# Taking the transpose and value steps of prompt attention two groups at a time

## The chip, the cores and the metric

The kernel runs on one core of a Trainium2 chip. The metric is the device time of the whole launch in microseconds, as the median of several runs. One execution was also profiled; all rows of the trace below come from it. Times in a row are counted from the first instruction of that execution.

## What is computed

One inference step of a hybrid decoder layer for a prompt of 2048 tokens and a group of 8 short samples. Three mixers stand side by side: A, a dilated sliding-window attention with 6 heads of 64; B, a gated linear recurrence (RG-LRU) after a short convolution; C, a chunked gated recurrence (HGRN2). The change touches only A, and only for the prompt:

```python
def dilated_branch_prompt(q, k, v, window, dilation):
    ...
    scores = jnp.einsum('brnqhd,brnkhd->brnhqk', qb, kband, ...) * (dh ** -0.5)
    ...
    scores = jnp.where(valid[:, None], scores, -jnp.inf)
    mx = jnp.max(scores, axis=-1, keepdims=True)
    p = jnp.exp(scores - mx)
    l = jnp.sum(p, axis=-1, keepdims=True)
    o = jnp.einsum('brnhqk,brnkhd->brnqhd', p, vband.astype(jnp.float32)) / jnp.swapaxes(l, 3, 4)
```

Three such branches (window, dilation) = (128, 1), (512, 4), (2048, 16) are merged with weights proportional to their denominators. Everything is in float32.

## The kernel before, in words

The program has two parts. `front` normalizes the input, projects it and runs the two recurrences. `attend_project` computes the attention of the prompt (and, at its start, the recurrence C of the samples and the last value columns), then the attention of the samples and the output projection. The change is in `attend_schedule`, which writes out by hand one list of steps, `order`. Each engine runs through that same list in one loop and does its own part of each step, so the list fixes the order on every engine's queue. Waits between engines are semaphores.

The steps that matter here:

- **u** (192 of them, 32 for each head): the scores of one tile of 128 queries against 128 to 512 keys. TensorE does two matmuls (L2545, L2546) into one of three PSUM banks (`a_s`); VectorE adds the mask and takes the row's extreme (L2306), which frees the bank: score step n waits at L2537 until step n-3 was shifted. ScalarE then takes the exponential and the row sum (L2167). In a head, unit k of 32 is: four of 128 keys, four near ones (128 or 256), then four of 256, four near, four of 384, four near, four of 512, four near.
- **w, x, z** (once for each head): the statistics of the far keys are sent across partitions. After the last exponential of the head VectorE makes `a_exch` (L2230), TensorE spreads it with eight small matmuls (x, L2594), VectorE and ScalarE merge, TensorE spreads the result (z, L2602), and VectorE copies the weights (L2367). GpSimd then scales the head's probabilities with them (L2082), in ten instructions.
- **t** (108 of them, 18 for each head): one group of four 128x128 blocks of probabilities is transposed by TensorE (L2613) into one of two PSUM banks (`a_t`). ScalarE copies three groups of four to SBUF (L1677), VectorE the fourth (n with n % 4 == 3, L1679), into one of four buffers `a_pt`.
- **o** (108): the four transposed blocks of a group are multiplied with the values (L2636), in 128*64 tiles of TensorE, two column halves side by side; 8 matmuls in the trace for 4 blocks. It waits for the copy of its group.
- **f** (12): VectorE multiplies a finished half of a head with its gate (L2377) and SyncE stores it.
- **pw** (9): ScalarE rounds a slab of the output weights (L2178), VectorE takes the rest (L2383). SyncE loads the slabs into four buffers; slab n+4 is loaded when pw n is over. **pt**: TensorE transposes a tile of the mixed rows for the projection (L2696), after it was loaded from DRAM.

The groups trail the scores: a head's groups begin LEAD = 11 score steps after its last score step. After each one or two score steps from there on, the inner function `turn` appends one t step, the o step of two groups before, and an f step where one is due. So in the middle of the kernel the list reads, for one head's stretch: u81 u82 t22 o20 u83 t23 o21 u84 u85 t24 o22 u86 u87 t25 o23. After the last score step (u191) come the 24 groups that are left, with the steps x, z, pw and pt between them.

Of the kernel before, what the change touches and what calls it, by code (L numbers as in the profile page):

```python
# [1388 lines left out]
def project_schedule():  # L1389

    first = [32 * b // 10 + 4 for b in range(NB)]
    at = {}
    for b, s in enumerate(first):
        for step, kind in enumerate(("sk", "sm", "so")):
            at[s + step] = (kind, b)  # L1400
    order = []
    for s in range(2 * NTILE):
        i, h = s // 2, s % 2
        kind, b = at.get(s, ("", 0))
        if h == 0 and i:
            order.append(("pt", i + 1))
        if at.get(s + 1, ("",))[0] == "sk":
            order.append(("sr", at[s + 1][1]))
        if kind == "sk":
            order.append(("ss", b))  # L1410
        order.append(("pp", s))
        if s == 0:
            order.append(("pt", 1))
        if s == 1:
            order.append(("sq", 0))
        if kind:
            order.append((kind, b))
        if at.get(s - 1, ("",))[0] == "so":
            order.append(("sb", at[s - 1][1]))
        order.append(("pe", s))  # L1420
        if s < 3:
            order.append((("si", "sj", "sl")[s], 0))
        tail = [("sc", b), ("sx", b), ("sn", b)] if kind == "sk" else []
        done = [("pf", i), ("pg", i), ("ph", i)] if h else []
        order += [x for pair in itertools.zip_longest(tail, done) for x in pair if x]
    n = 2 * NTILE
    return order + [("pp", n), ("pe", n), ("pp", n + 1), ("pe", n + 1)] + [(k, NTILE) for k in ("pf", "pg", "ph")]
# [10 lines left out]
def block_keys(i, far, m):  # L1438

    if far:  # L1440
        return list(range(i + 1))
    return [j for j in (NC * i + m, NC * i + m - 1) if j >= 0]
# [6 lines left out]
def last_group(groups, h, i):  # L1449
    return max(t for t, (g, blocks) in enumerate(groups) if g == h and any(b[0] == i for b in blocks))  # L1450


def attend_schedule():

    units = [(h, i, far, m) for h in range(NH) for i in range(SB) for far in (1, 0) for m in range(NC)]
    groups = []
    for h in range(NH):
        rows = [[(i, far, a, j) for i in both for far in range(2) for a in range(NC) for j in block_keys(i, far, a)] for both in LANES]
        blocks = [b for pair in itertools.zip_longest(*rows) for b in pair if b]
        groups += [(h, blocks[b:b + 4]) for b in range(0, len(blocks), 4)]  # L1470
    per, gper = len(units) // NH, len(groups) // NH
    ends = [max(last_group(groups, h, both[step]) for both in LANES) for h in range(NH) for step in range(2)]
    halves = [(h, j) for j in range(J0, XTILES) for h in ("va", "vb")]
    order, made = [], 0
    for step in ("ha", "va", "vb", "hb", "va", "hp", "qa", "ht", "hc", "vb", "hd", "va", "vb", "hx", "va"):
        order.append(halves.pop(0) if step[0] == "v" else (step, 0))
    order.append(("qa", 1))
    hgrn = {0: [("hk", 0), ("he", 0)], 1: [("hz", 0), ("hp", 1)], 2: [("ht", 1), ("hp", 2)], 3: [("ht", 2), ("hp", 3)],
            4: [("ht", 3), ("hj", 0)], 5: [("hj", 1)], 9: [("lk", 1)], 11: [("hq", 0), ("hv", 0)],
            12: [("hr", 0), ("hv", 1)], 13: [("hn", 0)]}  # L1480
    for h in range(NH):
        hgrn.setdefault(5 + h, []).append(("ho", h))
        if h < NH - 2:
            hgrn.setdefault(6 + h, []).append(("hj", h + 2))
    later = {2: [("hu", 0)], 3: [("hu", 1), ("hv", 2)], 5: [("hu", 2), ("hv", 3)], 6: [("hu", 3), ("hv", 4)],
             7: [("hu", 4), ("hv", 5)], 9: [("hu", 5)], 10: [("hs", 0)]}

    def turn():
        nonlocal made
        order.append(("t", made))  # L1490
        if made >= 2:
            order.append(("o", made - 2))
        if made - 3 in ends:
            order.append(("f", ends.index(made - 3)))
        made += 1

    for u in range(len(units)):
        h, k = u // per, u % per
        order.append(("u", u))
        if h == 0 and k % 2:  # L1500
            order += hgrn.get(k // 2, [])
            if halves:
                order.append(halves.pop(0))
            if k + 1 == per:
                assert not halves
                order += [("ve", 0), ("qa", 2), ("qa", 3)]
        if h == 1:
            order += later.get(k, [])
        if h and h + 1 < NH:
            order += {2: [("lk", h + 1)], 12: [("qn", 2 * h + 2)], 18: [("lv", 1)] * (h == 1), 22: [("qn", 2 * h + 3)]}.get(k, [])  # L1510
        if h and k in (1, 4):
            order.append(("x" if k == 1 else "z", h - 1))
        if k + 1 == per:
            order.append(("w", h))
        done = u + 1 - per - LEAD
        while done >= 0 and made < done // per * gper + done % per * gper // per + 1:
            turn()
    left = (NH - 1) * gper - made
    for n in range(left):
        turn()  # L1520
        if n in (1, 3):
            order.append(("x" if n == 1 else "z", NH - 1))
    order.append(("pl", 0))
    for n in itertools.count():
        if 4 <= n < 4 + KM:
            order.append(("pw", n - 4))
        if n == 11:
            order.append(("pm", 0))
        if n == 16:
            order.append(("pt", 0))  # L1530
        if made == len(groups):
            break
        turn()
    order += [("o", made - 2), ("o", made - 1), ("f", len(ends) - 1)]
    return units, groups, ends, order + project_schedule()


def attend_project(nc, sem, io, con, zf, zt, zs, mt, mab):

    units, groups, ends, order = attend_schedule()
    PER = len(units) // NH
    NCH = NH // 2
# [1256 lines left out]
```

## Time and profile before

| | |
|---|---|
| Median of 3 runs | 1688.76 us (1685.87 to 1689.35) |
| Profiled execution, first to last instruction | 1690.4 us |
| Its own time beside that span | not given apart from the span |
| TensorE matmul busy | 1588.9 us, 94% |
| TensorE weight load busy | 1345.8 us, 80% |
| VectorE busy | 976.2 us, 58% |
| ScalarE busy | 823.9 us, 49% |
| GpSimd busy | 628.9 us, 37% |
| Mean granted TensorE clock | 0.969 |
| Stretch with t and o steps | 1180 to 1376 us |

The busy shares are means over stages with different limits; what the change is worth is read from the stretch from 1180 to 1376 us. PE is TensorE's matmuls, PEld its weight loads, which overlap the matmuls; DVE is VectorE, ACT ScalarE, POOL GpSimd, SP SyncE. A matmul's duration in the trace covers its way through the array, so neighbours overlap: the distance from start to start says what one costs. "Idle before" in square brackets is how long the engine stood still ahead of the row, with what ended it; "issue" there means that nothing was waited for that the profile shows.

### The profile page before, as it was taken

The page shows a single profiled execution, that of the slowest core. Times are in us where ns is not written, and L with a number is a line of the kernel's source. Part 1 is how long each engine was busy: PE and PEld are TensorE (multiplying, and loading weights), DVE is VectorE, ACT ScalarE, POOL GpSimd, SP SyncE. Part 2 cuts the span into 40 slices and gives each one's busy share as a digit, 9 for nine tenths or more (in the row PEclk, how much of TensorE's full clock was granted, in tenths as well). Part 3 has the DMA queues.
Part 4 walks back from the last instruction along what each step waited for, and adds up shares of the span by engine and source line. Part 5 has one row for each costly group of instructions (what it writes and reads, how often), then busy time and mean ns, then how long its engine had stood idle before and what let it go on. Part 6 is the DMA issues. An engine that isn't in the chain of part 4 may idle for free. (4 is left out here: it accounts for less than half of the span.)

```text
span 1690.4 us, 38531 instructions
## 1 busy us (share of the span) xinstructions
PE 1588.9 (94%) x15345; PEld 1345.8 (80%) x15345; DVE 976.2 (58%) x2066; ACT 823.9 (49%) x1603; POOL 628.9 (37%) x754
## 2 busy tenths in 40 slices
PE   6999998899999999999999998899999888999997
PEld 5988887889988888878888787886777667777775
DVE  3436763433377777677676776325666556555652
ACT  4426876212256555566767776244777631111110
POOL 1102221200076666666666665203645602121110
PEclk9999998999999999999999999897999989999999
DMA  6310111124412212121110211447993284775651
GB/s 212 114 51 29 34 39 59 50 73 135 141 38 62 57 36 79 41 75 30 56 46 26 67 31 43 118 112 178 239 237 85 78 258 127 247 229 189 208 171 47
DMA packets 196287, 175.27 MB, mean 104 GB/s; under 512 B 84915, under 2 KB 180686, under 8 KB 193806
## 3 DMA queue, kind: packets, MB, share of 16 engines
q1 hardware_dynamic: 196110, 172.82, 35.6%
q8 instruction: 122, 2.00, 0.5%
q14 instruction: 55, 0.45, 0.1%
HBM read 123.18 MB, written 52.84 MB: 104 GB/s over the span
## 5 line engine op out<-in xcount | busy, mean ns | idle before, releaser
L49 PE MATMUL f_bank<-c_ht,c_whi 128*128 128x384 f32 (+1 forms) x864 | 321.0, 372 | 5.7 <-DVE c_wlo L893 5.7
L51 PE MATMUL f_bank<-c_ht,c_wlo 128*128 128x384 f32 (+1 forms) x864 | 303.3, 351 | 0.0
L50 PE MATMUL f_bank<-c_ht,c_whi 128*128 128x384 f32 (+1 forms) x864 | 302.9, 351 | 0.0
L842 ACT ACTIVATE f_scr<-f_scr 128x384 f32<-128x384 f32 (+1 forms) x210 | 114.0, 544 | 206.3 <-POOL f_scr L617 206.2
L1056 DVE TENSOR_TENSOR f_scr<-f_scr 128x192 f32<-128x192 f32 (+1 forms) x210 | 105.4, 502 | 137.4 <-ACT f_scr L842 137.1
L49 PEld LDWEIGHTS f_bank<-c_ht,c_whi 128*128 128x128 f32 x864 | 162.7, 188 | 21.4 <-DVE c_wlo L893 6.5
L50 PEld LDWEIGHTS f_bank<-c_ht,c_whi 128*128 128x128 f32 x864 | 163.2, 189 | 9.7 <-issue 1.1
L51 PEld LDWEIGHTS f_bank<-c_ht,c_wlo 128*128 128x128 f32 x864 | 163.0, 189 | 9.4
L616 POOL TENSOR_TENSOR f_scr<-f_scr 128x192 f32<-128x192 f32 (+1 forms) x210 | 134.6, 641 | 40.7 <-PE f_tps L1240 37.8
L1047 DVE COPY_PREDICATED f_scr<-f_scr,f_tps 128x384 f32<-128x384 int32 (+1 forms) x210 | 130.6, 622 | 18.1 <-PE f_tps L1240 9.5
L49 PE MATMUL a_s<-a_whi,a_mhi 128*128 128x512 f32 (+1 forms) x306 | 125.8, 411 | 4.5 <-DVE a_y L2471 4.5
L50 PE MATMUL a_s<-a_wlo,a_mhi 128*128 128x512 f32 (+1 forms) x306 | 122.4, 400 | 0.0
L642 POOL TENSOR_SCALAR f_scr<-f_scr,c_lbl 128x384 f32<-128x384 f32 (+1 forms) x30 | 43.5, 1451 | 209.7 <-ACT f_scr L808 209.7
L1240 PEld LDWEIGHTS f_tps<-f_scr 128*32 128x32 f32 (+1 forms) x5184 | 74.3, 112 | 40.0 <-issue 30.4
L1240 PE MATMUL f_tps<-f_scr 128*32 128x32 f32 (+1 forms) x5184 | 95.6, 200 | 2.5 <-DVE f_scr L1056 2.4
L2102 POOL TENSOR_TENSOR a_small<-a_small,c_mhalf 128x1 f32<-128x1 f32 (+1 forms) x17 | 9.3, 544 | 235.4 <-DVE a_small L2475 235.4
L49 PE MATMUL f_bank<-c_whi,c_ht 128*128 128x384 f32 x256 | 92.3, 360 | 2.2 <-DVE c_wlo L897 2.2
L51 PE MATMUL f_bank<-c_whi,c_ht 128*128 128x384 f32 x256 | 88.2, 344 | 0.0
L50 PE MATMUL f_bank<-c_wlo,c_ht 128*128 128x384 f32 x256 | 88.2, 344 | 0.0
L49 PE MATMUL f_bank<-c_htail,c_whi 128*128 128x448 f32 x216 | 84.3, 390 | 0.0
L51 PE MATMUL a_s<-a_whi,a_mlo_a 128*128 128x512 f32 (+1 forms) x204 | 82.0, 402 | 0.0
L50 PE MATMUL f_bank<-c_htail,c_whi 128*128 128x448 f32 x216 | 79.3, 367 | 0.0
(401 smaller groups left out, 3816.2 us busy)
## 6 DMA issues: line engine op xcount, KB each, us to landing
f_wraw<-in_w_in SPq DMA_DIRECT2D x27, 512.0 KB, 4.0
zs<-f_stage SPq DMA_DIRECT2D x48, 192.0 KB, 2.4
a_k<-in_ck SPq DMA_DIRECT2D x48, 192.0 KB, 5.7
a_v<-in_cv SPq DMA_DIRECT2D x48, 192.0 KB
f_scr<-in_xp SPq DMA_DIRECT2D x16, 512.0 KB, 4.2
a_x<-in_xp SPq DMA_DIRECT2D x16, 512.0 KB, 5.6
out_y_prompt<-a_y SPq DMA_DIRECT2D x16, 512.0 KB, 2.9
zt<-f_stage SPq DMA_DIRECT2D x38, 192.0 KB, 1.8
```

Source lines behind the costliest of these rows:

```text
L49: nc.tensor.matmul(out, w_hi, m_hi, start=start, stop=False)
L50: nc.tensor.matmul(out, w_hi, m_lo, start=False, stop=False)
L51: return nc.tensor.matmul(out, w_lo, m_hi, start=False, stop=stop)
L616: G.tensor_tensor(d[:, :, hs:], b[:, :, hs:], r, ALU.subtract)
L642: G.tensor_scalar(key[:, :n], key[:, :n], lbl[:, 1, h:h + 1], None, ALU.mult).then_inc(S["gated"], 1)
L842: A(lev[i % 3][:, :n], lev[i % 3][:, :n], ACT.Exp).then_inc(S["expd"], 1)
L1047: V.copy_predicated(attn[:, :n].rearrange("p (j t) -> p j t", t=P), m.bitcast(I32).unsqueeze(1).to_broadcast([P, nt, P]), lp[x % 2][:, :n] ...
L1056: V.tensor_tensor(e[:, :, hs:], e[:, :, hs:], q[:, :, hs:], ALU.mult).then_inc(S["xlev"], 1)
L1240: mm = nc.tensor.matmul(lp[x % 2][k0:k0 + w, queries], left[:, keys], right[:, queries], start=True, stop=True)
L2102: G.tensor_tensor(s[:, 2:3], s[:, 1:2], con["mhalf"][:rows_of(n), 0:1], ALU.pow).then_inc(Z["rstd"], 1)
```

## The change

`turn` handles two groups at once: two t steps, then the two o steps of the two groups before, then the f steps due. It is called half as often. The number and kind of instructions stay the same, and so do the buffers; only the order in the queues changes. The scores that stood between two single turns now stand together, so three or four score steps come in a row: u81 u82 u83 t22 t23 o20 o21 u84 u85 u86 u87 t24 t25 o22 o23.

```diff
+    assert gper % 2 == 0
+
     def turn():
         nonlocal made
-        order.append(("t", made))
+        order.extend(("t", made + x) for x in range(2))
         if made >= 2:
-            order.append(("o", made - 2))
-        if made - 3 in ends:
-            order.append(("f", ends.index(made - 3)))
-        made += 1
+            order.extend(("o", made - 2 + x) for x in range(2))
+        order.extend(("f", ends.index(n)) for n in (made - 3, made - 2) if n in ends)
+        made += 2
 
     for u in range(len(units)):
...
-        while done >= 0 and made < done // per * gper + done % per * gper // per + 1:
+        while done >= 0 and made + 1 < done // per * gper + done % per * gper // per + 1:
             turn()
     left = (NH - 1) * gper - made
     for n in range(left):
-        turn()
+        if n % 2 == 0:
+            turn()
         if n in (1, 3):
             order.append(("x" if n == 1 else "z", NH - 1))
...
         if made == len(groups):
             break
-        turn()
+        if n % 2 == 0:
+            turn()
     order += [("o", made - 2), ("o", made - 1), ("f", len(ends) - 1)]
```

Around the exchange of a head (here head 2) the list before is u93 u94 t29 o27 u95 w2 u96 t30 o28 u97 x2 u98 t31 o29; after the change it is u91 u92 u93 u94 t28 t29 o26 o27 f2 u95 w2 u96 u97 x2 u98 t30 t31 o28 o29. Near the end the list before is t94 o92 pw1 t95 o93 pw2 t96 o94 pw3 t97 o95; after the change it is pw0 t94 t95 o92 o93 pw1 pw2 t96 t97 o94 o95 pw3 pw4.

## Rows read from the trace of the kernel before

**Rows 1.** Busy time by stage: head 1's groups, the fourth of four heads, the tail.
```profile
core 0: us, PE busy (x) PEld busy (x) DVE busy (x) ACT busy (x) POOL busy (x), PEclk, DMA share, GB/s
1180.01:1203.61 23.60, 23.52 (x187) 18.92 (x187) 13.48 (x50) 17.92 (x53) 13.77 (x7) 0.89 0.97 217
...
1299.54:1331.66 32.12, 32.12 (x301) 24.86 (x301) 20.07 (x83) 25.52 (x80) 16.72 (x10) 1.00 0.08 18
1331.66:1376.34 44.68, 33.88 (x296) 24.39 (x295) 25.52 (x33) 18.30 (x28) 17.68 (x10) 0.81 0.55 176
```

**Rows 2.** Waits from 1203 to 1330 us: total, times, longest.
```profile
PEld a_o L2636 <- issue: 11.4, 68, 0.2
...
PEld a_s L2545 <- DVE a_sn L2306: 3.4, 20, 0.2
```

**Rows 3.** Timeline of TensorE: start, duration, instruction; a turn between near scores.
```profile
1209.19 0.38 PE L2545 MATMUL a_s<-a_khi,a_qn 128*128 128x256 f32 x1
...
1209.54 0.28 PE L2545 MATMUL a_s<-a_khi,a_qn 128*128 128x256 f32 x1
...
1209.77 0.60 PE L2613 MATMUL a_t<-c_ident,a_pf 128*128 128x128 f32 x4
1210.30 0.66 PE L2636 MATMUL a_o<-a_pt,a_vf 128*64 128x128 f32 x8
1210.89 0.38 PE L2545 MATMUL a_s<-a_khi,a_qst 128*128 128x256 f32 x1
```

**Rows 4.** Timeline: a turn without scores, and the last three o steps.
```profile
1342.51 0.65 PE L2613 MATMUL a_t<-c_ident,a_pnb 128*128 128x128 f32 x4
...
1343.68 0.44 PE L2613 MATMUL a_t<-c_ident,a_pnb 128*128 128x128 f32 x2
...
1373.51 2.79 PE L2636 MATMUL a_o<-a_pt,a_vf 128*64 128x128 f32 x22
```

**Rows 5.** Timeline: from a score's start to the start of its exponential, 256 keys.
```profile
1304.71 0.38 PE L2545 MATMUL a_s<-a_khi,a_qn 128*128 128x256 f32 x1
...
1305.90 0.51 ACT L2167 ACTIVATE a_pnb<-a_pnb,a_sn 128x256 f32<-128x256 f32 x1
```

**Rows 6.** The same with 512 keys.
```profile
1229.88 0.50 PE L2545 MATMUL a_s<-a_khi,a_qst 128*128 128x512 f32 x1
...
1231.57 0.73 ACT L2167 ACTIVATE a_pf<-a_pf,a_sf 128x512 f32<-128x512 f32 x1 [0.87 <-DVE a_sf L2306]
```

**Rows 7.** Timeline: a head's last score, its exponential, the exchange on VectorE and TensorE.
```profile
1297.31 0.39 PE L2545 MATMUL a_s<-a_khi,a_qn 128*128 128x256 f32 x1
...
1298.57 0.49 ACT L2167 ACTIVATE a_pnb<-a_pnb,a_sn 128x256 f32<-128x256 f32 x1
...
1299.19 0.29 DVE L2230 TENSOR_TENSOR a_exch<-a_sf,a_quarter 128x128 f32<-128x128 f32 x1 [0.72 <-ACT a_pnb L2167]
...
1299.54 0.27 PE L2594 MATMUL a_x<-a_exch,a_unit_row 128*32 128x32 f32 x8
```

**Rows 8.** Timeline of the tail: VectorE, TensorE.
```profile
1345.95 7.67 DVE L2383 TENSOR_TENSOR a_wlo<-a_wraw,a_whi 128x1024 fp32r<-128x1024 f32 x2 [2.18 <-ACT a_whi L2178]
...
1353.54 0.68 DVE L1679 COPY a_pt<-a_t 128x512 f32<-128x512 f32 x1
...
1354.37 0.45 PE L2613 MATMUL a_t<-c_ident,a_pnb 128*128 128x128 f32 x1 [5.92 <-DVE a_pt L1679]
```

**Rows 9.** The chain that ended last, from 1354 to 1363 us.
```profile
1354.22 1.14 DVE a_wlo L2383
...
1355.38 4.58 DMA a_wraw<-in_w_out
...
1362.21 1.16 DVE a_oa L2377
```

**Rows 10.** Timeline of TensorE in the projection: small matmuls after a wait.
```profile
1475.96 1.19 PE L2513 MATMUL a_o<-a_selm,a_far_rows 128*96 128x16 f32 x12 [1.69 <-DVE a_far_rows L2418]
```

**Rows 11.** The stretch behind Rows 10, columns as in Rows 1.
```profile
1478.60:1482.00 3.40, 3.40 (x10) 2.26 (x8) 1.76 (x5) 0.44 (x1) 0.00 (x0) 0.51 1.11 330
```

## The prediction, made before the result was known

> **What bounds the kernel now.** I read the busy time by stage first. The change acts between 1180 and 1376 us only. In the four heads between (heads 2 to 5, some 32.1 us each, one of them shown) the matmul row is full, ACT is busy 25.5 us, DVE 20.1 us [rows 1]. The chain of waits of that stretch names TensorE's steps for most of its length. A full matmul row says little, since neighbours overlap, so I went on to the waits of the stretch and to the timeline. The waits show nearly nothing that another engine causes: the gaps ahead of the score steps are put down to DVE, but none is over 0.2 us, and the same gap stands 68 times ahead of an o step with no cause at all [rows 2]. So TensorE is the bound there, and it has a gap of its own at each change of kind.
>
> The timeline prices this gap. The pace of a transposed block is 0.105 us: four blocks last 0.65, two last 0.44, half the difference [rows 4]. An o step of four blocks has the same pace. One whole turn without scores takes 1.17 us (1342.51 to 1343.68), its eight blocks 0.85; so two changes of kind cost 0.31 us [rows 4]. Between scores it shows in another shape: t to o takes 0.53 us where the blocks need 0.43, which is 0.10; o to u takes 0.59, which is 0.16; and the first score behind o takes 0.35 until the next starts, a later one 0.23, which is 0.12 more [rows 3]. That makes 0.38 us for each turn. Going from u to t costs nothing that I can see (0.23 us, as between two scores). The last three o steps stand in one row of 22 matmuls that lasts 2.79 us [rows 4]; at the half clock of that place 11 pairs need 2.3, so no gap lies inside it: an o step directly behind another is free. I take the same for t behind t, which the trace never shows at full clock.
>
> **What the change removes.** Of two turns' gaps one remains: 0.37 us less for each pair. Scheduled work stays the same. Heads 2 to 5 hold 36 pairs, nine a head: 3.3 us a head.
>
> **What it adds, first the banks.** Two scores in a row become three or four, and there are three score banks. The fourth score of a run waits until DVE has shifted the first. From the start of a score to the start of its exponential takes 1.19 us with 256 keys [rows 5], 1.69 with 512 [rows 6], and the bank is free at the same moment as the exponential may start. TensorE would like to start the fourth at 0.35 + 0.23 + 0.23 = 0.81 us, so it waits 0.38 and then loses up to 0.12 as the first score behind a gap does: 0.5 us. In the run k = 27 to 30 the first score has 512 keys and the others 256: wanted at 1.05 (0.35 + 0.23 for the first, then 0.46), free at 1.69: 0.64 and 0.1, say 0.75. A head has four such runs (k = 6 to 9, 13 to 16, 20 to 23, 27 to 30): 3 x 0.5 + 0.75 = 2.25 us. The other runs have three scores, or an exchange between, and wait for nothing. The bounds: 0 if the banks come free in time, 3 us if DVE is behind with a copy or an f step (0.69 and 1.1 us) at that time. I take 2.25, from the rows.
>
> A page speaks on this place. The Trainium skill, Perfetto Trace Analysis, section Optimizing Tensor Performance, Matmuls, wants independent matmul groups to rotate through different PSUM banks, so that the evacuation of one overlaps the matmuls of the next. By it the run of four over three banks is a fault of the change; the trace agrees as far as no bank wait shows before, where runs have two scores. The same page, section Identifying the Most-Contended Engine, takes the weight loads' busy share as the better measure of TensorE: by it 7.3 of the 32.1 us of a head stand open [rows 1], and a better order could take up to four times that; the gaps priced above are some 6.8 us of it.
>
> **Then the exchange.** Step x needs the head's last exponential and DVE's spread. From the start of the last score to x pass 2.23 us (1297.31 to 1299.54), with ACT and DVE directly behind each other on the way [rows 7]. Before, a score, a t step, an o step and another score fill this time on TensorE. After the change only three scores stand between: about 0.7 us. So TensorE waits 1.5 us at x, once a head, in heads 2 to 5 (x1 to x4). Bounds: 1.2, and 2.5 if ACT is behind with exponentials. DVE's merge behind it is then as late as before against x; step t of the second pair behind it waits for ACT's copy some 0.4 us, where it waited 0.3 before: 0.1 more. Behind the waiting x on TensorE stand one score and the next pair; nobody but ACT and DVE waits for these.
>
> Sum for a head: -3.3 + 2.25 + 1.5 + 0.1 = +0.5 us; four heads: +2.0 us. The work that TensorE had in the gaps between is what hid the chains; now it is late at those chains instead.
>
> **Head 1's groups** (1180 to 1203 us, 23.6 us, clock 0.89 [rows 1]): five pairs with both kinds save 5 x 0.37 = 1.9; of its runs of four one falls into half clock, where TensorE takes twice as long and the bank is free in time, two cost 0.5 and 0.75. Net -0.6 us. There is no x behind it beside the one counted.
>
> **The tail** (44.7 us [rows 1]). Between w5 and x5 two pairs of steps stay, so x5 is covered; 0.3 us less until x5, and with it until z5 and GpSimd's scaling. The pairs until t90 wait for that scaling anyhow, nothing. Then DVE: before, the copy of group 95 stood behind pw0 and pw1, which took 7.67 us together, and TensorE waited 5.92 us for it [rows 8]. Now it stands behind pw0 only, some 3.8 us earlier. But the end of the tail hangs on the slabs: DVE's pw2, the load of a slab 4.58 us, ACT, DVE, then f10 at 1362.21, its store and the load for step pt [rows 9]. pw1 took 3.8 us where the same work takes 1.14 [rows 9], so it ended late for another reason than its queue (GpSimd is in its last scalings until then); the copy of 0.6 us now fits into that time. pw2 starts 0.6 us earlier, and all behind it. Last, two changes of kind fewer at half clock behind pt: 0.4 to 0.7 less. Sum -0.3 - 0.6 - 0.4 = -1.3 us; bounds 0 (DVE and ACT are met otherwise) and -4 (TensorE keeps its clock, since it waits 2 us and not 6).
>
> **Sum.** +2.0 - 0.6 - 1.3 = +0.1 us against the profiled execution of 1690.4 us, which lies 1.6 us over the median 1688.76. I carry the difference to the median: 1688.9 us.
>
> **Rivals.** (1) The chains stay hidden: banks free in time and x covered. For it speaks that DVE is busy only 20 of 32 us. Then only the gaps count: -36 x 0.37 - 1.9 - 1.3 = -16.5, 1672 us. If the banks are free and only x waits, 4 x 2.25 + 1.25 = 10.3 us are gone from the forecast: 1678.6. If all losses (4 x 3.85 + 1.25 = 16.7) are half as large, 1680.6. Against it the 1.19 and 1.69 us [rows 5, 6], which hold no queueing. Chance of this family 0.25.
>
> (2) The clock. In the projection twelve small matmuls behind a wait of 1.69 us [rows 10] are followed by 3.4 us at a granted clock of 0.51, the 1.2 GHz level [rows 11]. The wait at x is 1.5 us with eight small matmuls behind it, and the 0.75 us wait of the run before lies 3 us ahead. If the clock falls there in each of four heads, 3.4 us at half pace lose up to 1.7 each, 6.8 in all: 1695.7. [...] Against it: around x stand full scores, in the projection nearly nothing. Chance 0.15. The Trainium skill, TensorE: Matmul & The Clock Gate, Part 1, has the throttled state as the default and activity as what lifts it, so it leaves both outcomes open.
>
> (3) ACT is behind. It has 25.5 us of work in 32.1 [rows 1], its copies of a pair now come after the exponentials of a run of four. If each pair's t steps wait 0.2 us for it, 36 pairs make +7: 1696. Chance 0.08.
>
> (4) The gap belongs to each step's wait and not to the change of kind, so pairing removes none: +0.5 + 3.3 a head, 1703 us. The 22 matmuls in one row speak against it [rows 4], and the free step from u to t. Chance 0.04.
>
> **The numbers.** The forecast has 0.48. A difference of 0.2%, 3.4 us, is about what a measurement of this kernel can tell from no change. Faster by more: rival 1, 0.25, and 0.03 of the forecast, where its bounds add up on the low side: 0.28. Slower by more: rivals 2 to 4, 0.27, less 0.05 for a clock that falls in one head or two only, and 0.02 of the forecast: 0.24. Within: 0.48. Range: from 1678, where only x waits, up to 1697, where rivals 2 and 3 end; outside lie the full rival 1 (about 0.1) and rival 4. The likeliest case's own range is 1685 to 1692.5.
>
> **What would show it.** In the profile after: waits of the score line for DVE of 0.4 to 0.7 us, four a head; a wait of x for DVE of about 1.5 us, in four heads; the gaps "issue" ahead of o halved, from 68 to about 36 in heads 2 to 5; a head from x to x of 32 to 33 us; the copy of group 95 at about 1350 us and TensorE's wait of 5.9 us there down to 2 or 3; f10 about 0.6 us earlier against x5. Wrong I would be if x is not waited for, if the fourth score starts at once, or if the granted clock falls below 1 between 1203 and 1330 us.

## The result

The changed kernel takes 1703.1 us, against 1688.2 for the kernel before in the same session: a ratio of 1.009, 95% interval 1.007 to 1.011, so 15 us slower. The forecast was 1688.9 with a range of 1678 to 1697. The time lies outside it.

The profiled execution of the changed kernel has a span of 1705.1 us (before: 1690.4). TensorE does the same matmuls in it and is busy 1580.5 us instead of 1588.9, and idle for longer. Line numbers from the changed functions on are 3 higher than before (L2616 is the t step, L2639 the o step, L2548 the score, L2597 x, L2085 GpSimd's scaling, L2057 its copy of the queries); in the experiments they move on by what each edit adds.

I cut both traces at the steps x, of which each head has one, and at the first matmul of the projection. All times in us:

| stretch | before | after | difference | forecast |
|---|---|---|---|---|
| start to x0 | 1161.9 | 1159.9 | -2.0 | 0 |
| x0 to x1 (head 1) | 41.7 | 46.8 | +5.1 | -0.6 |
| x1 to x2 | 32.1 | 36.4 | +4.3 | +0.5 |
| x2 to x3 | 31.7 | 34.3 | +2.6 | +0.5 |
| x3 to x4 | 32.1 | 34.5 | +2.4 | +0.5 |
| x4 to x5 | 32.1 | 32.7 | +0.6 | +0.5 |
| x5 to the projection (tail) | 44.6 | 41.1 | -3.5 | -1.3 |
| projection to the end | 314.2 | 319.4 | +5.3 | 0 |

The last head is the forecast's head. Four stretches ahead of it are not: they are 5.7, 3.8, 2.1 and 1.9 us over the forecast. The last row is a matter of that one execution: in the eleven kernels that follow this stretch takes 312.9 to 316.6 us with nothing changed in it. The first row is no result either: one kernel below has the order of before up to this point and reaches x0 at 1156.1.

Busy time of the changed kernel by stage, columns as in [rows 1]: head 1's groups, head x1 to x2, head x4 to x5, the tail.

```profile
core 0: us, PE busy (x) PEld busy (x) DVE busy (x) ACT busy (x) POOL busy (x), PEclk, DMA share, GB/s
1183.09:1206.69 23.60, 21.00 (x171) 18.08 (x171) 12.48 (x44) 15.96 (x47) 14.41 (x8) 0.87 1.01 224
1206.69:1243.10 36.41, 31.44 (x294) 26.04 (x294) 19.98 (x83) 24.46 (x79) 18.69 (x12) 0.95 0.76 201
1311.87:1344.55 32.68, 31.26 (x314) 26.09 (x314) 20.43 (x83) 24.81 (x80) 16.71 (x10) 1.00 0.06 15
1344.55:1385.78 41.23, 28.25 (x296) 22.37 (x295) 25.44 (x33) 18.49 (x28) 18.66 (x10) 0.92 0.59 187
```

POOL's count tells the two kinds of head apart: 12 instructions where a head copies queries for the next one, 10 in the last head, which copies none. Next the waits from 1206 to 1345 us (heads 2 to 5), where [rows 2] had 68 gaps without a cause and nothing over 0.2 us; first TensorE's, then two of its queue for weight loads:

```profile
PE a_x L2597 <- DVE a_exch L2233: 5.1, 4, 1.3
PE a_t L2616 <- POOL a_pnb L2085: 4.8, 3, 2.3
PE a_s L2548 <- DVE a_sn L2309: 2.8, 12, 0.2
PE a_s L2548 <- DVE a_sf L2309: 2.0, 4, 0.5
...
PEld a_s L2548 <- issue: 6.4, 36, 0.3
PEld a_o L2639 <- issue: 6.2, 36, 0.3
```

Three of these the forecast has: x waits in four heads, the fourth score of a run waits 12 + 4 times, and 36 gaps ahead of o instead of 68. One it has not: the second line. TensorE's t step waits for GpSimd, three times here and once more for 5.8 us in head 1. GpSimd's timeline in head 2 shows why; first the kernel before, then the changed one:

```profile
1207.77 0.97 POOL L2082 TENSOR_TENSOR a_pna<-a_pna,a_wt 128x128 f32<-128x128 f32 x2 [13.99 <-PE a_s L2546]
...
1224.43 2.03 POOL L2054 CAST a_qn<-a_qst 128x1024 fp32r<-128x1024 f32 x2
```
```profile
1214.54 1.04 POOL L2057 CAST a_qn<-a_qst 128x1024 fp32r<-128x1024 f32 x1 [17.04 <-DMA a_qst<-zs]
1215.54 0.97 POOL L2085 TENSOR_TENSOR a_pna<-a_pna,a_wt 128x128 f32<-128x128 f32 x2
```

Each engine takes its instructions from the same written order. Pairing moved the head's first t step from ahead of the step qn (unit 12) to behind it. GpSimd's ten scalings belong to that first t step, and qn waits for the transfer of the next head's queries. Before, GpSimd scaled first, 4.2 us behind x1, and copied at 1224.4 without a wait. Now it stands at the copy until 1214.5, with the scalings behind it, which start 8.9 us behind x1. And behind a long wait TensorE's clock is down. Timeline of TensorE in the changed kernel, and the stretch behind the wait with its granted clock (columns as in [rows 1]):

```profile
1219.42 0.33 PE L2616 MATMUL a_t<-c_ident,a_pna 128*128 128x128 f32 x1 [2.31 <-POOL a_pnb L2085]
...
1221.05 1.98 PE L2639 MATMUL a_o<-a_pt,a_vf 128*64 128x128 f32 x14
```
```profile
1219.42:1223.00 3.58, 3.58 (x23) 2.92 (x23) 0.69 (x1) 0.60 (x1) 3.58 (x3) 0.55 0.67 153
```

Eight blocks and eight pairs take 3.5 us here (1219.42 to 1222.95) and 2.0 at full clock: the wait costs its 2.3 us and 1.5 more. The next two heads differ. In x2 to x3 the t step waits only 0.53 us for GpSimd, and most of the +2.6 us is a lower clock behind x2, which experiment 1 has too; in x3 to x4 it waits 1.97 us, and the clock stays at 1.00 behind it.

### The profile page after: what moved, and what is told of

Same layout as the page of the kernel before. It is cut to its first block and busy times, and to the rows that moved or that the text cites. A ratio compares the mean times of both kernels' runs of the same rounds, so it can differ in the third digit from the quotient of the medians.

```text
span 1705.1 us, 38531 instructions
## 1 busy us (share of the span) xinstructions
PE 1580.5 (93%) x15345; PEld 1347.4 (79%) x15345; DVE 974.7 (57%) x2066; ACT 821.2 (48%) x1603; POOL 628.3 (37%) x754
## 5 line engine op out<-in xcount | busy, mean ns | idle before, releaser
L616 POOL TENSOR_TENSOR f_scr<-f_scr 128x192 f32<-128x192 f32 (+1 forms) x210 | 134.3, 640 | 40.3 <-PE f_tps L1240 37.7
L1240 PEld LDWEIGHTS f_tps<-f_scr 128*32 128x32 f32 (+1 forms) x5184 | 74.5, 112 | 39.7 <-issue 30.4
L49 PE MATMUL f_bank<-c_htail,c_whi 128*128 128x448 f32 x216 | 84.4, 391 | 0.0
L51 PE MATMUL f_bank<-c_htail,c_wlo 128*128 128x448 f32 x216 | 79.4, 368 | 0.0
```

The source lines that it names most:

```text
L49: nc.tensor.matmul(out, w_hi, m_hi, start=start, stop=False)
L51: return nc.tensor.matmul(out, w_lo, m_hi, start=False, stop=stop)
L616: G.tensor_tensor(d[:, :, hs:], b[:, :, hs:], r, ALU.subtract)
L1240: mm = nc.tensor.matmul(lp[x % 2][k0:k0 + w, queries], left[:, keys], right[:, queries], start=True, stop=True)
```

## The experiments

Where a quoted expectation speaks of a first kernel, it is that of experiment 1 (1688.6 us); "the head with the lock-step pairs" is head 1. Each ratio is to the kernel before, measured beside that run; its 95% interval stands behind it.

**1. The copy behind the scalings again.** The changed kernel, with one number of the order changed.

```diff
-            order += {2: [("lk", h + 1)], 12: [("qn", 2 * h + 2)], ...
+            order += {2: [("lk", h + 1)], 13: [("qn", 2 * h + 2)], ...
```

> The changed kernel with one entry of the order moved: in each head the first copy of the next head's queries stands one place later in the order, so that GpSimd's queue holds the scalings of the head's first transposed group ahead of the copy, as it does before the change. Theory 1, GpSimd's queue: the copy waits for its DMA with the scalings behind it; the wait in front of TensorE's first group of a head goes, and with it the lower clock behind it. x0 to x1 falls from 46.8 us to about 41.3, the next three heads from 36.4, 34.3 and 34.5 us to about 32.7 each, and the time from 1703.1 us to about 1690 (1687 to 1693 with what the stretch behind the heads does). Theory 2, the loss lies in the waits at x and in the longer runs of scores, and the copy is only late beside them: the heads stay at 34 to 36 us and the time within 2 us of 1703.

Measured: 1688.6 us, ratio to before 0.9993 (0.9982 to 1.0004). x0 to x1 takes 40.3 us, the heads 32.3, 33.5, 32.3 and 32.7. Theory 1 holds (x0 to x1 even 1 us below it, one head 0.8 above), theory 2 falls. The whole loss of the change was this place in GpSimd's queue. GpSimd's timeline in head 2 (x1 is at 1200.48) and TensorE's waits in the four heads:

```profile
1204.36 0.97 POOL L2085 TENSOR_TENSOR a_pna<-a_pna,a_wt 128x128 f32<-128x128 f32 x2 [12.77 <-DVE a_wt L2370]
...
1221.02 2.02 POOL L2057 CAST a_qn<-a_qst 128x1024 fp32r<-128x1024 f32 x2
```
```profile
PE a_x L2597 <- DVE a_exch L2233: 5.1, 4, 1.3
PE a_s L2548 <- DVE a_sn L2309: 2.7, 12, 0.2
PE a_s L2548 <- DVE a_sf L2309: 2.0, 4, 0.5
```

The waits for GpSimd are gone, the others stay. The 33.5 us head has a slow stretch of clock behind its x; more on that below. With the place of the copy restored, pairing itself shows no gain that is clear of noise: the interval holds 1.

**2. The copy ahead, nothing paired.** The kernel before, with the same step moved the other way.

```diff
-            order += {2: [("lk", h + 1)], 12: [("qn", 2 * h + 2)], ...
+            order += {2: [("lk", h + 1)], 10: [("qn", 2 * h + 2)], ...
```

> The kernel before, with its order of transposes and products untouched, and only the copy of the queries moved ahead of the first transposed group of each head in GpSimd's queue. Theory 1, GpSimd's queue: the head's first groups come late although no transposes are paired; the heads that have such a copy grow by 2.4 to 4.3 us each as in the changed kernel (9.3 us for three of them, up to 5 us more for the head with the lock-step pairs), so about 1697 to 1702 us. Theory 2, the loss comes from the pairing itself: no difference from the kernel before, 1688 us.

Measured: 1705.3 us, ratio 1.0098 (1.0076 to 1.0120). x0 to x1 takes 48.3 us, the heads 35.9, 33.9, 34.2 and, without a copy, 32.1. Theory 1 holds, 3 us above its range: x0 to x1 grew by 6.6 us, not by up to 5. TensorE waits for GpSimd's scaling up to 7.0 us:

```profile
PE a_t L2613 <- POOL a_pnb L2082: 12.8, 4, 7.0
```

The four kernels so far are a table of two by two, here as ratios to the kernel before: copy behind, 1 unpaired and 0.9993 paired; copy ahead, 1.0098 unpaired and 1.0090 paired. The copy's place is worth 16 us, pairing some 1 us less, which is within the intervals.

**3. Transpose, product, transpose, product.** As experiment 1, with another order inside each turn.

```diff
-        order.extend(("t", made + x) for x in range(2))
-        if made >= 2:
-            order.extend(("o", made - 2 + x) for x in range(2))
+        for x in range(2):
+            order.append(("t", made + x))
+            if made >= 2:
+                order.append(("o", made - 2 + x))
```

> The first kernel of this call with the order inside each turn of two groups changed from transpose, transpose, product, product to transpose, product, transpose, product. Runs of scores, the copy of the queries and the steps x and z stay. It separates the saving by pairing from everything else. If the gap belongs to each change between a transpose or product and its neighbour of the other kind, the turn pays 0.31 us more for each of some 54 turns, about 16 us beside the first kernel of this call: 1706 us. If the second transpose's inputs or the banks of its result decide, the two orders are within 3 us.

Measured: 1709.7 us, 1.0116 (1.0096 to 1.0136), 21 us over experiment 1. The first branch comes nearer; its 1706 us are 4 short. Timeline of TensorE in one such turn:

```profile
1252.32 0.60 PE L2617 MATMUL a_t<-c_ident,a_pf 128*128 128x128 f32 x4
1252.85 0.66 PE L2640 MATMUL a_o<-a_pt,a_vf 128*64 128x128 f32 x8
1253.44 0.55 PE L2617 MATMUL a_t<-c_ident,a_pf 128*128 128x128 f32 x3
1253.91 0.66 PE L2640 MATMUL a_o<-a_pt,a_vf 128*64 128x128 f32 x8
```

From the first t to the score behind the last o pass 2.18 us here (1252.32 to 1254.50), 2.29 in the next turn; a paired turn takes 0.97 + 1.02 to 1.03. So 0.2 to 0.3 us come back a turn, where 0.31 was expected. The heads lose more than their nine turns: 3.8, 4.5, 3.9 and 2.5 us against experiment 1. The granted clock of the four is 0.95, 0.91, 0.95 and 1.00: the last has only the gaps (9 x 0.2 to 0.3 = 1.8 to 2.7 us), the others lose clock besides (experiment 1 does so in one of them), with waits of up to 1.6 us at x.

**4. Pairs, singles, short runs.** The changed kernel with its turns placed by a list.

```diff
-    def turn():
+    def turn(w=2):
...
+    after_unit = {0: 1, 2: 1, 5: 2, 8: 2, 11: 2, 14: 2, 17: 1, 20: 2, 23: 2, 26: 2, 29: 1}
...
-        done = u + 1 - per - LEAD
-        while done >= 0 and made + 1 < done // per * gper + done % per * gper // per + 1:
-            turn()
+        if (u >= per + 11) and k in after_unit:
+            turn(after_unit[k])
```

> The changed kernel with the turns placed by a fixed list: seven turns of two groups and four of one in each head, so that no run of scores is longer than three, one single turn stands between the last score and x, and the queries' copy stays behind the first groups. If the sum of the prediction is made of independent terms (0.37 us saved per pair, 0.4 to 0.7 us lost per fourth score of a run, 1.3 us lost at each x), the saving stays without the two losses: 7 x 0.37 = 2.6 us in each of four heads, 10.4 us, 1.5 us in the first one and the 3.5 us of the last stretch ahead of the projection: about 1673 us. If groups of two hold the exponentials of ScalarE back or free the banks late, waits ahead of scores take it back: 1680 to 1690 us.

Measured: 1676.2 us, 0.9926 (0.9908 to 0.9944): 13.6 us faster than before, the fastest kernel of this study. The heads take 31.1, 30.4, 31.3 and 30.4 us at full clock, and the fourth score waits nowhere. It is 3 us short of the forecast, for a wait that was new:

```profile
PE a_x L2605 <- DVE a_exch L2233: 3.2, 4, 0.8
PE a_t L2616 <- POOL a_pnb L2085: 2.4, 1, 2.4
PE a_x L2597 <- DVE a_exch L2233: 2.0, 3, 0.8
```

The first line is z (L2605), which has a turn of one in front of it now and not of two. The second is in the tail.

**5. Those waits covered by a later x and z.** Three kernels: experiment 1 with x and z two units later, experiment 4 with both later, experiment 4 with z alone one unit later.

```diff
-        if h and k in (1, 4):
-            order.append(("x" if k == 1 else "z", h - 1))
+        xk, zk = (1, 4) if h == 1 else (3, 6)
+        if h and k in (xk, zk):
+            order.append(("x" if k == xk else "z", h - 1))
```
```diff
-        if h and k in (1, 4):
+        if h and k in (1, 5):
```

> The changed kernel with the queries' copy one place later (the first kernel of the first call, 1688.6 us) and besides, from head 2 on, the steps x and z two units later, so that a turn of two groups stands between the last scores and x. If the 1.27 us that TensorE waits at each of four x steps belong to that place alone, they go and nothing replaces them: 4 x 1.3 = 5.1 us, about 1683.5. If what waits moves on (z, or a later score of a run that has grown across the end of the head), the time stays within 2 us of 1688.6.

> The kernel with seven turns of two and four of one (1676.2 us) and, from head 2 on, x and z two units later. Its trace shows TensorE waiting 2.0 us in all at x and 3.2 us at z, both for the row of the exchange. If both waits are covered by the turns now ahead of them: 1676.2 - 5 = 1671 us. If the chain behind x and z is what counts (their results are needed by the row's writers of the next head), no change or some us more.

> The kernel with seven turns of two and four of one (1676.2 us), x where it was and z alone one unit later in each head, so that TensorE's 0.79 us wait at z in four heads is covered by one more unit of scores. If that wait is lost time: 1676.2 - 3.2 = 1673 us. If it moves on, as the waits at x and z did in the kernel that had both later, within 2 us of 1676.2.

Measured: 1685.3 us (0.9975, 0.9962 to 0.9988) for the first, 3.3 less than experiment 1; 1679.5 (0.9942, 0.9923 to 0.9961) and 1680.4 (0.9946, 0.9932 to 0.9960) for the others, no gain over 1676.2 and rather a few us more. Waits of TensorE, in the heads of the first kernel, then from 1200 to 1331 us of the second, last from x1 on in the third:

```profile
PE a_s L2549 <- DVE a_sn L2310: 3.1, 12, 0.3
PE a_t L2617 <- POOL a_pnb L2086: 2.6, 4, 0.8
PE a_s L2549 <- DVE a_sf L2310: 2.0, 4, 0.5
```
```profile
PE a_t L2617 <- POOL a_pnb L2086: 4.5, 5, 2.4
PE a_t L2617 <- ACT a_pt L1681: 2.8, 4, 0.7
```
```profile
PE a_s L2548 <- DVE a_sf L2309: 4.2, 4, 1.1
```

The waits at x and z are gone in the first two, and others have come. (The longest of the second, 2.4 us, is in the tail, where experiment 4 has it too; the other four are 0.2 to 0.9 us.) The row weights come out of x and, behind it, z; GpSimd can't scale without them, so a later x and z make the scalings, and the head's first near group, later. In the third, z waits for nothing, but the score now ahead of it, the fourth behind x, waits for its bank, up to 1.1 us in each of four heads. So the 5.1 us at x were worth 3.3 at most, since the heads of the first kernel also keep their clock, where experiment 1 loses some 1.6 us behind x2; the 5.2 us at x and z were worth nothing.

**6. Pairs in the tail alone.** The kernel before, with pairs only behind the last score.

```diff
-        turn()
+        if n % 2 == 0:
+            turn_two()
```

> The kernel before in all heads; only behind the last score are transposes and products taken two and two. If the 3.5 to 3.9 us by which the stretch from the last x to the projection is shorter in the kernels with pairs come from that stretch itself, the time is 1689.9 - 3.5 = 1686.4 us, and that stretch shows 40.7 to 41.1 us against 44.57. If they come from what the heads hand over (an earlier free engine, a full clock), the stretch stays at 44 to 45 us and the time at 1690.

Measured: 1686.2 us, 0.9983 (0.9971 to 0.9995), 3.3 us less than before's 1689.5; the stretch takes 41.6 us against 44.6. But experiment 2, whose tail is not paired, shows 41.3 us there too. The gain of the time is measured, its place isn't settled: a stretch comes from one trace, and an unpaired tail can be as short as a paired one.

**7. The load two units earlier.** The changed kernel, with lk at unit 0 instead of 2.

```diff
-            order += {2: [("lk", h + 1)], 12: [("qn", 2 * h + 2)], ...
+            order += {0: [("lk", h + 1)], 12: [("qn", 2 * h + 2)], ...
```

> The changed kernel with the copy of the queries left where the change puts it, ahead of the scalings, and the load that it waits for issued two units earlier in each head. If the delay is the copy's wait for that DMA, and not the copy's 1.04 us of work or its place as such, it shrinks by what the load gains, some 2 us in each of four heads and more where TensorE's clock then stays up: 1693 to 1698 us. If the transfer's landing is not what holds the queue, no change: 1703 us.

Measured: 1704.0 us, 1.0093 (1.0067 to 1.0118). This run decides nothing. SyncE's queue holds the load behind the store of a finished half (`mab`), which waits for VectorE's f step, and it went out 0.2 us ahead of x1, as in the changed kernel (1206.47, x1 at 1206.69; here x1 is at 1207.65):

```profile
1206.29 1.11 SPq L1953 DMA_DIRECT2D mab<-a_oa  x2
1207.44 1.24 SPq L1853 DMA_DIRECT2D a_qst<-zs  x2
```

I had moved a step past nothing: the second time in this case that a queue other than the one I looked at set the time.

**8. The copy in its new place, but waiting for no transfer.** The changed kernel; the first copy of a head reads the buffer of the head that is loaded already, and the load that overwrites this buffer waits for the copy.

```diff
-                    pool.wait_ge(q_in[h % 2], BASE + 32 * (h // 2 + 1))
+                    held = h - 1 if n % 2 == 0 else h
+                    pool.wait_ge(q_in[held % 2], BASE + 32 * (held // 2 + 1))
...
+                    if n % 2 == 0:
+                        src = near_queries(n - 2)[1]
...
+                    if n > 2:
+                        sp.wait_ge(S["q_near"], BASE + 2 * (n - 1) - 3)
                     load_split(n)
```

> The changed kernel with the copy of the next head's queries in the place that the change gives it, ahead of the scalings, but reading the head that is loaded already: it waits for no transfer (the near scores of half of the queries of heads 2 to 5 are then made from the wrong head's queries; all work and all transfers are kept). If the wait for the transfer holds the scalings up, the time goes to that of the kernel with the copy behind them, 1688.6 us, or up to 1692 with the copy's own 1.04 us still ahead of them in four heads. If the copy's place as such or its work is the cause, it stays at 1703.

Measured: 1695.9 us in the median, 1.004 (1.0016 to 1.0063), but no execution took this time: five took 1686.6 to 1691.8 us and five 1700.1 to 1703.9. The profiled one is of the upper group. In it the four heads take 32.3, 32.3, 32.3 and 33.9 us, so the wait for the transfer was what cost there (the 33.9 has a granted clock of 0.56 behind x4); but x0 to x1 takes 55.0 us. VectorE's and GpSimd's timelines in head 1:

```profile
1172.59 0.68 DVE L2352 TENSOR_TENSOR a_h_s<-a_h_s,a_h_gl 128x512 f32<-128x512 f32 x1
1175.05 1.39 DVE L2352 TENSOR_TENSOR a_h_s<-a_h_s,a_h_gl 128x512 f32<-128x512 f32 x1
1178.20 16.30 DVE L2352 TENSOR_TENSOR a_h_s<-a_h_s,a_h_gl 128x512 f32<-128x512 f32 x1
```
```profile
1174.83 1.03 POOL L2062 CAST a_qn<-a_qst 128x1024 fp32r<-128x1024 f32 x1
...
1177.23 2.89 POOL L2090 TENSOR_TENSOR a_pnb<-a_pnb,a_wt 128x512 f32<-128x512 f32 x2
...
1186.67 6.31 POOL L2090 TENSOR_TENSOR a_pf<-a_pf,a_wt 128x2048 f32<-128x2048 f32 x2
1192.93 1.03 POOL L2062 CAST a_qn<-a_qst 128x1024 fp32r<-128x1024 f32 x1
```

A product of VectorE that takes 0.68 us ends only when GpSimd's whole run ends, 16.3 us later, and TensorE waits 14.3 us behind it. The lower group has no trace. A new theory, then, for the last run: this meeting makes the two groups.

**9. The same from head 2 on.** Experiment 8, with head 1's copy waiting for its transfer again, which brings the scalings behind the product.

```diff
-                    held = h - 1 if n % 2 == 0 else h
+                    held = h - 1 if n % 2 == 0 and h > 2 else h
...
-                    if n % 2 == 0:
+                    if held < h:
                         src = near_queries(n - 2)[1]
```

> The kernel whose copies wait for no transfer, with head 1's copy put back as the change has it, waiting for its transfer (from head 2 on the near scores of half of the queries of heads 3 to 5 are still made from the wrong head's queries). Theory: the two groups of times of that kernel, 1687 to 1692 and 1700 to 1704, differ by one VectorE instruction of head 1, the product on the state of the short sequences, that met GpSimd's ten scalings there and took 16.3 us; here the scalings start behind it again. Then the times form one group, head 1 costs what it does in the changed kernel (x0 to x1 some 47 us), the next three heads 32.3 us each, and the time is 1703.1 - 8.3 = 1694.8 us. If the two groups come from something else in these kernels, they remain; if the three heads' gain came from head 1's late end, it goes and the time is 1703.

Measured: 1693.5 us, 1.0020 (1.0008 to 1.0031), and the times form one group, 1690.2 to 1696.2. x0 to x1 takes 47.2 us, the next three heads 32.3 each, the last 33.9, and all six products 0.69 us. What the theory forecast has come. That the meeting makes the two groups is not shown beyond that, since no trace of experiment 8's lower group exists. In heads 2 to 4 the wait for the transfer costs 9.6 us by the medians (1703.1 to 1693.5), 8.3 by the heads of the traces; some 1.2 to 1.6 of the 8.3 are the lower clock, which stands behind x2 in the changed kernel and behind x4 here. The copy's own microsecond costs nothing there, for GpSimd is idle at that time. The rest of the 14.5 us that experiment 1 wins, 4.9 us, belongs to head 1, where the traces show 6.9 (47.2 against 40.3).

## Why the prediction was wrong

**The step that failed** is in "What the change removes": "Scheduled work stays the same." It does, but it changes places, and I followed its order on TensorE, VectorE and ScalarE alone. The step t is also GpSimd's: its scalings hang on the first t of a head. Pairing moved that t from ahead of qn to behind it, in four heads. In the trace of before qn waited for nothing, so no wait there shows the cost; the order of the steps per engine, and a look at when the transfer of a_qst lands, would have. In head 2 of before it went out at 1206.30 and took 8.4 us to land in the median of its two parts, while the scalings began at 1207.77. For head 1 I wrote that there is no x behind it beside the one counted, took -0.6, and saw +5.1; for three of the heads +0.5, and saw +2.4 to +4.3 (with the clock behind x2 in one of them). None of the four rivals had this mechanism. Rival 4 gave 1703 us, the time that came, but its reason is false: the gaps did go, as experiment 3 shows by bringing them back.

**The terms for the heads** can be read from experiment 1, which has the change without this step, and from the last head of the changed kernel.

- Gaps at changes of kind: forecast 0.37 us a pair. A paired turn takes 0.97 + 1.03, against twice 0.53 + 0.59 and one more first score at 0.12 [rows 3]: 0.36 us. Right; that t behind t is free, which I had assumed, is seen at last.
- The fourth score of a run: forecast 0.50 and 0.75 us. TensorE's timeline in experiment 1 shows the third score's last matmul and the fourth's first. The second line should start 0.12 us behind the first and starts 0.51 behind; with the first score's 0.11 that is 0.50:

```profile
1240.72 0.28 PE L2549 MATMUL a_s<-a_klo,a_qst 128*128 128x256 f32 x1
1241.23 0.39 PE L2548 MATMUL a_s<-a_khi,a_qst 128*128 128x256 f32 x1 [0.23 <-DVE a_sn L2309]
```

- In the run with 512 keys the step is 0.78 us, so 0.66 + 0.1. Right, and at the places named.
- The wait at x: forecast 1.5 us in four heads. In the changed kernel the second matmul of the last score ahead of x starts at 1310.32, and x waits:

```profile
1311.52 0.29 DVE L2233 TENSOR_TENSOR a_exch<-a_sf,a_quarter 128x128 f32<-128x128 f32 x1 [0.67 <-ACT a_pnb L2170]
...
1311.87 0.27 PE L2597 MATMUL a_x<-a_exch,a_unit_row 128*32 128x32 f32 x8 [1.27 <-DVE a_exch L2233]
```

- From that matmul to x pass 1.55 us instead of some 0.1, so 1.4 are lost. Right.
- Sum: forecast +0.5 a head and +2.0 for four; the last head of the changed kernel has +0.6, and the four of experiment 1 have +2.8, of which 1.6 belong to the next point.

**Rival 2, the clock at x,** came true in one head of four, as the chance of 0.15 and the deduction for "one head or two" had left room for. The two matmul steps behind x2 took 1.81 + 1.82 us where the same take 0.99 + 1.03 behind x3, which followed a wait of the same 1.27 us:

```profile
1243.30:1247.20 3.90, 3.90 (x34) 3.32 (x26) 2.62 (x15) 1.96 (x8) 0.00 (x0) 0.56 0.99 218
```

In experiment 1 it is the same head (33.5 us, granted clock 0.56 over the 3.9 us behind x2). But it is not a matter of that head: with the same waits of 1.27 us at x1 to x4, experiments 8 and 9 show it behind x4 alone (0.56 and 0.57), and experiment 7 behind x3 and x4 (0.63 and 0.57). Of 20 such waits in five traces, six were followed by it. What picks the place stays open.

**Rival 1** fell as a family: banks and x both wait. The terms add up in experiment 4, too, where runs of three and a turn ahead of x take the waits away: against experiment 1 its four heads take 7.5 us less, of which 1.6 are the clock of the point above. For the other 5.9 the terms give 9.0 (banks) + 3.7 (x, 0.5 of 1.4 us left) - 3.0 (two pairings fewer a head) - 3.2 (z) = 6.5.

**Head 1's groups** without the copy's wait: -1.4 us from x0 to x1 in experiment 1, forecast -0.6. **The tail:** forecast -1.3, bound -4, seen -3.5 in the stretch. VectorE's timeline there:

```profile
1357.96 1.28 DVE L2386 TENSOR_TENSOR a_wlo<-a_wraw,a_whi 128x1024 fp32r<-128x1024 f32 x1 [2.38 <-PE a_t L2616]
1359.16 0.68 DVE L1682 COPY a_pt<-a_t 128x512 f32<-128x512 f32 x1
1359.76 9.99 DVE L2386 TENSOR_TENSOR a_wlo<-a_wraw,a_whi 128x1024 fp32r<-128x1024 f32 x4
1369.68 0.68 DVE L1682 COPY a_pt<-a_t 128x512 f32<-128x512 f32 x1
```

The copy of group 95 (1359.16, 14.6 us behind x5) did come earlier, by 7.3 us and not 3.8: before it stood 21.9 behind x5 [rows 8]. What I missed is the next one, of group 99. Between the two now stand four slabs, and TensorE waits 5.4 us there, where it waited 5.9 for group 95: the wait has moved and not shrunk. The chain, as [rows 9]:

```profile
1363.71 3.78 DVE a_wlo L2386
1367.51 3.56 DMA a_wraw<-in_w_out
...
1373.32 1.16 DVE a_oa L2380
```

f10 stands 28.8 us behind x5 and stood 30.6 behind it: the same slab's load went out 0.75 us earlier against x5 (forecast 0.6), and took 3.56 us and not 4.58. The clock of the tail is at 0.92 and not 0.81. Experiment 2, with the tail unpaired, has the load at 3.59 us, f10 at 28.8 and the stretch at 41.3. So the -3.5 isn't shown to be the pairs', and that the sum came near the bound is no proof of my steps. That pw1 took 3.8 us "for another reason than its queue" has its reason now, in the last section.

**Without the overlooked step** the forecast is 1688.9 us, and experiment 1, which is that case, took 1688.6. That they meet so closely is partly luck: by the one trace the heads came out 0.8 us over their term, head 1 0.8 and the tail 2.5 under theirs.

## What to carry to other kernels

When steps are regrouped in a written order that several engines follow, list for every engine, GpSimd and the DMA queues among them, which of its steps passed which, and look for the one that waits for a transfer: a queue in order turns its wait into everyone's. A gain on the busiest engine is real only as far as no chain of the others was hidden in it: here 13 us of gaps gave 1 to 2 us, which is not clear of noise, until the turns were placed so that no run outlasts the three banks and something stands ahead of x (1676.2 us). And a wait that is covered by moving its step later can come back at whoever needed the step's result.

## What was not expected of the hardware

- VectorE's product of two SBUF tensors (0.68 us) took 16.3 us beside GpSimd's run of scalings in experiment 8: seven scalings and a copy of GpSimd's went by before it. In the eight other kernels with the scalings beside it (before is one) the same product takes 1.35 to 1.52 us, and 0.69 alone. In those eight the last of the six starts 0.93 to 0.94 us behind the start of a 128x512 scaling, in experiment 8 0.97 us; whether these hundredths decide was not tested. The times of experiment 8 form two groups 12 us apart. By the Trainium skill, SBUF — State Buffer, section SBUF: two separate sides, VectorE with two SBUF inputs and GpSimd share a pair of ports that one holds for its whole instruction while the other is blocked; the trace agrees on who is blocked, but the block outlasted eight instructions of GpSimd. What decides that is open.
- The same meeting is in the tail, before [rows 8] and after: two slabs' products take 3.8 to 4.0 us each and not 1.2 while GpSimd scales 128x2048. In the changed kernel the first slab's product starts 0.15 us ahead of these scalings and takes 1.28; before it started 0.7 behind their start and took 3.98. That is read from the rows, not tried by itself.
- In the changed kernel TensorE's granted clock falls to the 1.2 GHz level behind waits of 2.3 and 5.8 us (0.55 and 0.50 over the 3.6 us behind them), and behind one of 1.27 us once in four. But it stays at 1.00 over the 3.6 us behind a wait of 1.97 us (at 1289.8), so the length of the wait alone doesn't tell.
